# Row order of the expert weights and of the router's input, in a transformer block with 64 experts

## The chip, the core and the metric

The kernel runs on one core of a Trainium2 chip. The metric is the device time of one launch in microseconds (us). Before the change the median of three runs is 2787.24 us (2785.03 to 2787.96). The other cores of the chip are idle.

## What is computed

The input is 1024 tokens of 1024 numbers, all in float32. A first layer (an RWKV group, a sparse attention group and a memory group) and a second mixer (retention and convolution) are followed by a routed feed-forward layer, and only that layer is touched by the change. In short, for each token:

```
h2     = rms_norm(x1, norm2_w)                  # 1024 numbers
logits = h2 @ [router_g | router_e] + bias      # 8 group and 64 expert logits
e1, e2 = the two best experts of the best group, with two gates g1, g2
y      = sum over the two: g * ( silu(h2 @ w_gate[e]) * (h2 @ w_up[e]) ) @ w_down[e]
out    = rms_norm(x1 + y, final_norm_w)
```

`w_gate[e]` and `w_up[e]` are 1024 x 512, `w_down[e]` is 512 x 1024: each is 2 MB, and 64 experts have three each, 403 MB in all. With 2048 pairs of token and expert there are about 32 tokens to an expert, and a block holds up to 64.

## The kernel before, in words

The program is written by hand for each engine (`pe_...`, `act_...`, `dve_...`, `pool_...`, `sp_...`), with semaphores between them, and runs in stages. The change touches the last three.

**Router** (`dve_router`, `pe_router`). Token tile by token tile (8 tiles of 128) TensorE does the output projection of the mixer, VectorE adds it to the residual and writes the normalised tile `h2` (line 2439). SyncE stores `h2` to DRAM as `h2d`, each token as two rows of 512. TensorE transposes `h2` (line 2357) and multiplies it by the router weights `rw`. Line 2439 writes `h2` in a permuted order: of the 1024 numbers of a token, number `8 n + c` goes to place `128 c + n`. The slice `c` of 128 neighbours thus holds the numbers `c, 8 + c, 16 + c, ...`, which is the order in which the rows of the gate and up weights lie over the partitions: `(p c) n -> p (c n)` gives partition `p` the rows `8 p` to `8 p + 7`, one stretch of 16 KB in DRAM.

**Tables**. VectorE, TensorE and GpSimd build the lists of tokens of each expert.

**Experts** (`sp_experts`, `pe_experts`, `act_experts`, `dve_experts`, `pool_experts`). All loads of weights ("chunks" of 2 MB) are issued by SyncE in one order: gate, up, down of expert 0, then of expert 1, and so on, 192 chunks into 7 buffers. Chunk `k` waits until TensorE has finished with chunk `k - 7`, and the waits are taken in order, so that a chunk whose buffer is free waits behind one whose buffer isn't. The first two are issued in the router stage, five more when that stage's memory is free. GpSimd gathers the tokens of a block (`xg`, 64 tokens as 128 rows of 512) and scatters the results (`ys`). In each turn of its loop TensorE does, in this order:

- gate(e) and up(e) in `hidden`, 8 products each;
- `turn_x(e+1)`: four transposes of `xg`. The tile that is turned is the stationary operand, so each has one weight load (LDWEIGHTS) of 128 columns;
- down(e-1), 8 products;
- `turn_h(e)`: eight small products that turn the gate and the up result, `Gs[0]` and `Gs[1]`, which are again the stationary operand. A float32 product is run as two passes, each with a weight load, so these are 16 loads of 128 columns.

Between them ScalarE copies the gate result from PSUM to `Gs[0]` (line 2692, through the helper on line 229) and the turned tokens to `xT2` (line 2682, same helper), VectorE copies the up result to `Gs[1]` (line 2717). Both copies into `Gs` permute: number `4 n + c` goes to place `128 c + n` (`rows_of_wd`), which is the order of the rows of `w_down` over the partitions.

After the experts a stage ("over") handles blocks beyond 64, which are none here, and the final stage loads `yb`, adds, normalises and stores.

Of the kernel before, what the change touches and what calls it, by code (L numbers as in the profile page):

```python
# [14 lines left out]
ALU = mybir.AluOpType  # L15
# [141 lines left out]
def program(nc, inp, out):  # L157
# [48 lines left out]
    def s(name):  # L206
        if name not in sems:
            if name in LATER:
                old, left = LATER[name]
                sems[name] = Signal(s(old).sem, s(old).base + left)  # L210
            else:
                sems[name] = Signal(ctx.enter_context(nc.semaphore(name)), 0)
        return sems[name]
# [4 lines left out]
    def mm(pe, o, l, r, start, stop):  # L218
        return pe.e.matmul(o, l, r, start=start, stop=stop)  # L219
# [8 lines left out]
    def copy(act, o, i):  # L228
        return act.e.activation(o, i, ACT.Copy)  # L229
# [17 lines left out]
    def C(name, a=0, n=128):  # L247
        return con[:, CON[name] + a:CON[name] + a + n]

    ident = C("id")  # L250
# [292 lines left out]
    def four(a):  # L543
        return a.rearrange("p (a n) -> p a n", a=4)
# [1693 lines left out]
    xres = sb("xres", [128, 8, D], c=high)  # L2238
    NCH = 7
    wch = [sb(f"wch{i}", [128, 4096], c=high) for i in range(2)]  # L2240
# [34 lines left out]
    n2b = sb("n2b", [128, D], c=c8_)  # L2275
    rw = sb("rw", [128, 8, 72], c=c8_)
    rb_ = sb("rb_", [128, 72], c=c8_)
    junk5 = sb("junk5", [128, D], c=c8_)
    h2 = [sb(f"h2{i}", [128, D], c=c8_) for i in range(3)]
# [19 lines left out]
    def chunk_loaded(k):  # L2299
        return s(f"chunk_slot{k % NCH}"), 16 * (k // NCH + 1)  # L2300

    def sp_chunk(sp, k):
        if k >= NCH:
            e, n = (k - NCH) // 3, (k - NCH) % 3
            u = ps[("gate", "up", "down")[n], e]
            sp.wait_ge(u.full, u.v)
        e, n = k // 3, k % 3
        src = inp[("wg", "wu", "wd")[n]][e].rearrange("(p c) n -> p (c n)", p=128)
        sp.e.dma_start(wch[k % NCH], src).then_inc(chunk_loaded(k)[0].sem, 16)  # L2309

    def wo2_load(eng, first):
        for c in range(first, 8, 2):
# [6 lines left out]
    def h2_stored(j):  # L2319
        return s(f"h2_slot{j % 3}"), 16 * (j // 3 + 1)  # L2320
# [94 lines left out]
    def dve_router(dve):  # L2415
        dve.wait_ge(s("norm2_gain"), 16)
        dve.wait_ge(s("router_b"), 16)
        dve.wait_ge(s("con2"), 16)
        for j in range(8):
            m = small[:, 16 + j:17 + j]  # L2420
            dve.wait_ge(s(f"x{j}"), 32)
            for n in range(2):
                ns = slice(n * 512, (n + 1) * 512)
                u = ps["out2", j, n]
                dve.wait_ge(u.full, u.v)
                dve.e.tensor_tensor(xres[:, j, ns], xres[:, j, ns], u.t[:, :], ALU.add).then_inc(u.free.sem, 1)
            if j:
                dve_route(dve, j - 1)
            dve.wait_ge(s("res2_sq"), j + 1)
            dve.e.tensor_scalar(m, m, 1.0 / D, 1e-6, ALU.mult, ALU.add).then_inc(s("res2_mean").sem, 1)  # L2430
            dve.wait_ge(s("res2_root"), j + 1)
            dve.e.reciprocal(m, m).then_inc(s("res2_scale").sem, 1)
            dve.wait_ge(s("res2_scale"), j + 1)
            if j >= 3:
                dve.wait_ge(*h2_stored(j - 3))
                u = ps["h2T", j - 3, 1]
                dve.wait_ge(u.full, u.v)

            dve.e.scalar_tensor_tensor(h2[j % 3].rearrange("p (c n) -> p n c", c=8), xres[:, j, :].rearrange("p (n c) -> p n c", c=8),
                                       m, n2b.rearrange("p (n c) -> p n c", c=8), ALU.mult, ALU.mult).then_inc(s("h2").sem, 1)  # L2440
        dve_route(dve, 7)

    def dve_route(dve, j):
# [145 lines left out]
    Gs = [sb(f"Gs{i}", [128, 512], c=c11) for i in range(2)]  # L2589
# [13 lines left out]

    def turn_x(pe, o, x):
        for q in range(4):
            t = pe.e.transpose(o[:, q * 128:(q + 1) * 128], x[:, q * 128:(q + 1) * 128], ident)  # L2606
        return t

    def hidden(pe, o, w, xt_):
# [6 lines left out]

    def turn_h(pe, o, g):
        for c in range(4):
            t = mm(pe, o[:, c * 64:c * 64 + 64], g[:, c * 128:(c + 1) * 128], C("id2", 0, 64), True, True)
        return t  # L2620

    def rows_of_wd(u_):

        return u_.rearrange("p (n c) -> p c n", c=4)

    def down(pe, o, w, h_):
        for c in range(4):
# [10 lines left out]
    def sp_experts(sp):  # L2638
        for k in range(2, 3 * NEXP):
            sp_chunk(sp, k)  # L2640
# [35 lines left out]
    def act_turn_x(act, e):  # L2676
        u = ps["xT", "expert", e]
        act.wait_ge(u.full, u.v)
        if e >= 2:
            w = ps["up", e - 2]  # L2680
            act.wait_ge(w.full, w.v)
        copy(act, xT2[e % 2][:, :, :], four(u.t[:, :])).then_inc(u.free.sem, 1)

    def act_experts(act):
        act_turn_x(act, 0)
        for e in range(NEXP):
            u = ps["gate", e]
            act.wait_ge(u.full, u.v)
            if e:
                w = ps["hT", e - 1]  # L2690
                act.wait_ge(w.full, w.v)
            copy(act, four(Gs[0][:, :]), rows_of_wd(u.t[:, :])).then_inc(u.free.sem, 1)
            if e + 1 < NEXP:
                act_turn_x(act, e + 1)
            u = ps["hT", e]
            act.wait_ge(u.full, u.v)
            if e >= 2:
                w = ps["down", e - 2]
                act.wait_ge(w.full, w.v)
            act.e.activation(sg[e % 2][:, :, :], u.t[:, :].rearrange("p (a n) -> p a n", a=8)[:, 0:4, :],  # L2700
                             ACT.Silu).then_inc(s("gate_half").sem, 1)

    def dve_down(dve, e):
        u = ps["down", e]
        dve.wait_ge(u.full, u.v)
        if e >= 2:
            dve.wait_ge(*scattered(e - 2))
        dve.e.tensor_scalar(ys[e % 2][:, :], u.t[:, :], gat[:, e:e + 1], None, ALU.mult).then_inc(u.free.sem, 1)  # L2708

    def dve_experts(dve):  # L2710
        for e in range(NEXP):
            u = ps["up", e]
            dve.wait_ge(u.full, u.v)
            if e:
                w = ps["hT", e - 1]
                dve.wait_ge(w.full, w.v)
            dve.e.tensor_copy(four(Gs[1][:, :]), rows_of_wd(u.t[:, :])).then_inc(u.free.sem, 1)  # L2717
            if e:
                dve_down(dve, e - 1)
            u = ps["hT", e]  # L2720
            dve.wait_ge(s("gate_half"), e + 1)
            dve.e.tensor_tensor(sg[e % 2][:, :, :], sg[e % 2][:, :, :], u.t[:, :].rearrange("p (a n) -> p a n", a=8)[:, 4:8, :],
                                ALU.mult).then_inc(u.free.sem, 1)
        dve_down(dve, NEXP - 1)
# [38 lines left out]
    obank = ps.tiles  # L2763

    def sp_over(sp, n):
        sp.wait_ge(s("over_done"), n)
        for k_, name in enumerate(("wg", "wu", "wd")):
            v = sp.e.value_load(eid[n:n + 1, 0:1], min_val=0, max_val=NEXP - 1)
            src = inp[name][bass.ds(v, 1)]
            sp.e.dma_start(wch[k_], src.rearrange("a (p c) n -> p (a c n)", p=128)).then_inc(s(f"over_{name}").sem, 16)  # L2770

    def pool_over(pool, n):
        gather(pool, xg[0], NEXP + n).then_inc(s("over_x").sem, 16)
# [26 lines left out]
    def dve_over(dve, n):  # L2800
        dve.wait_ge(s("over_turned"), n + 1)
        dve.e.tensor_copy(xT2[0][:, :, :], four(obank[0][:, :])).then_inc(s("over_xT").sem, 1)
        dve.wait_ge(s("over_gate"), n + 1)
        dve.e.tensor_copy(four(Gs[0][:, :]), rows_of_wd(obank[1][:, :])).then_inc(s("over_gate_copied").sem, 1)
        dve.wait_ge(s("over_up"), n + 1)
        dve.e.tensor_copy(four(Gs[1][:, :]), rows_of_wd(obank[2][:, :])).then_inc(s("over_up_copied").sem, 1)
        dve.wait_ge(s("over_silu"), n + 1)
        dve.e.tensor_tensor(sg[0][:, :, :], sg[0][:, :, :], obank[3][:, :].rearrange("p (a n) -> p a n", a=8)[:, 4:8, :],
                            ALU.mult).then_inc(s("over_h").sem, 1)
        dve.wait_ge(s("over_down"), n + 1)  # L2810
        dve.e.tensor_scalar(ys[0][:, :], obank[4][:, :], gat[:, NEXP + n:NEXP + n + 1], None, ALU.mult).then_inc(s("over_y").sem, 1)
# [213 lines left out]
def layout(i):  # L3025
# [13 lines left out]
    a = {"x": i["x"][0], "mem": i["mem"][0]}  # L3039
# [27 lines left out]
    p, r = np.arange(128)[:, None], np.arange(128)[None, :]  # L3067
    for n in range(2):
        q = p % 64 + 64 * n
# [35 lines left out]
    a["n2"] = i["norm2_w_2"][0]  # L3105
    re = i["router_e_w_2"][0].transpose(1, 0, 2).reshape(1024, 64)
    rw = np.concatenate([i["router_g_w_2"][0], re], axis=1)
    a["rw"] = np.ascontiguousarray(rw.reshape(128, 8, 72))
    a["rb"] = np.concatenate([i["router_g_b_2"].reshape(-1), i["router_e_b_2"].reshape(-1)])
    a["wg"], a["wu"], a["wd"] = i["w_gate_2"][0], i["w_up_2"][0], i["w_down_2"][0]  # L3110
    a["fn"] = i["final_norm_w_2"]
# [1 line left out]
    p = np.arange(128)[:, None]  # L3113
# [30 lines left out]
```

## Time and profile before

| | us |
|---|---|
| median of three runs | 2787.24 |
| lowest and highest run | 2785.03, 2787.96 |
| time of the execution that was profiled | 2787.96 |
| its span in the trace | 2786.1 |

The profile page gives each engine's busy share (TensorE, "PE", 85%; its weight loads, "PEld", 55%; VectorE, "DVE", 28%; ScalarE, "ACT", 19%; GpSimd, "POOL", 21%) and, over 40 equal slices, what was busy when. One slice is 70 us, and the expert stage is the slices from 25 to 38. A busy share of TensorE says that products were in flight, not that it worked at its peak. The line "DMA" is the mean busy share of the core's 16 DMA engines; it can come out slightly over 1 where packets overlap. "L219" is line 219, the helper that issues nearly every product, and "L2309" the one that issues the chunks. Of shapes, `128*64 128x512` is a product with 128 rows and 64 columns of weights, through which 512 columns are moved. SPq, PEldq and the like are the queues of the engines.

### The profile page before, as it was taken

Reading aid. Unit: us, or ns where it says so; the run is one execution under the profiler, and the core shown is the slowest. Engines: PE = TensorE matmul, PEld = TensorE weight load, DVE = VectorE, ACT = ScalarE, POOL = GpSimd, SP = SyncE. Lnnn points to the kernel's source line nnn. Section 1 sums busy time; section 2 is a strip of 40 time slices with the busy share of each in tenths; the row PEclk is TensorE's granted clock in tenths of the full one; section 3 lists DMA queues with packets and bytes.
Section 4 is the critical chain, followed back from the end, with each engine's and each line's share of the span. In section 5 each row is a group of like instructions: output and inputs, shape, how many; then the busy total and the mean of one; then the engine's idle time right before and its main releaser. Section 6 shows DMA issues by size and latency. Waiting matters only on the chain. (4 is left out here: it accounts for less than half of the span.)

```text
span 2786.1 us, 42314 instructions
## 1 busy us (share of the span) xinstructions
PE 2370.5 (85%) x18624; PEld 1520.0 (55%) x18624; DVE 767.8 (28%) x1528; ACT 536.0 (19%) x1076; POOL 583.7 (21%) x366
## 2 busy tenths in 40 slices
PE   4899987888789999699999896988888888888881
PEld 4788865777567654488887454433333333333330
DVE  2311015553545533332323335111111111111114
ACT  2011123342255411111111121110010100100101
POOL 2433324331111111333322002111111111111113
PEclk9999988999799999899999997999999999999996
DMA  4122221002110011211111504899999999999994
GB/s 158 61 91 98 91 88 40 11 26 78 63 61 2 1 53 68 91 38 53 54 38 31 212 31 172 346 425 425 425 425 425 423 423 423 422 420 419 424 385 194
DMA packets 69647, 537.39 MB, mean 193 GB/s; under 512 B 13336, under 2 KB 13592, under 8 KB 43472
## 3 DMA queue, kind: packets, MB, share of 16 engines
q1 hardware_dynamic: 52720, 498.60, 43.6%
q10 hardware_dynamic: 6496, 19.19, 2.0%
q0 software_dynamic: 10240, 16.82, 1.6%
q8 instruction: 149, 2.44, 0.4%
q14 instruction: 42, 0.34, 0.0%
HBM read 503.08 MB, written 43.52 MB: 196 GB/s over the span
## 5 line engine op out<-in xcount | busy, mean ns | idle before, releaser
L219 PE MATMUL banks<-arena 64*64 64x64 f32 (+11 forms) x15392 | 1685.2, 346 | 271.3 <-DMA arena<-in_wu 84.5
L219 PEld LDWEIGHTS banks<-arena 64*64 64x64 f32 (+3 forms) x15392 | 953.2, 156 | 950.0 <-issue 684.1
L229 ACT ACTIVATE arena<-banks 128x512 f32<-128x512 f32 (+6 forms) x381 | 219.7, 587 | 1286.8 <-PE banks L219 561.5
L2600 POOL DMA_INDIRECT yb<-arena x64 | 65.1, 1018 | 841.2 <-DVE arena L2708 841.2
L2717 DVE COPY arena<-banks 128x512 f32<-128x512 f32 x64 | 44.3, 692 | 551.9 <-PE banks L219 551.9
L224 PE MATMUL banks<-r,w2s 128*128 128x512 f32 x448 | 177.4, 396 | 19.1 <-POOL w2s L1983 19.1
L224 PE MATMUL banks<-r,wlo 128*128 128x512 f32 x432 | 171.3, 397 | 7.2 <-POOL wlo L414 7.2
L225 PE MATMUL banks<-r,w2s 128*128 128x512 f32 x448 | 175.5, 392 | 0.0
L226 PE MATMUL banks<-r,w2s 128*128 128x512 f32 x448 | 175.1, 391 | 0.0
L226 PE MATMUL banks<-r,wlo 128*128 128x512 f32 x432 | 170.0, 394 | 0.0
L225 PE MATMUL banks<-r,wlo 128*128 128x512 f32 x432 | 169.8, 393 | 0.0
L1983 POOL TENSOR_TENSOR w2s<-arena,w2s 128x1024 fp32r<-128x1024 f32 x28 | 70.4, 2514 | 209.1 <-DVE w2s L1974 209.1
L2708 DVE TENSOR_SCALAR arena<-banks,arena 128x512 f32<-128x512 f32 x64 | 48.1, 751 | 222.3 <-PE banks L219 222.3
L224 PEld LDWEIGHTS banks<-r,w2s 128*128 128x128 f32 x448 | 84.9, 189 | 36.5 <-issue 19.4
L224 PEld LDWEIGHTS banks<-r,wlo 128*128 128x128 f32 x432 | 81.6, 189 | 25.9 <-POOL wlo L414 7.6
L226 PEld LDWEIGHTS banks<-r,w2s 128*128 128x128 f32 x448 | 84.8, 189 | 17.9
L225 PEld LDWEIGHTS banks<-r,w2s 128*128 128x128 f32 x448 | 84.9, 189 | 17.0
L1519 ACT ACTIVATE arena<-banks,arena 128x256 f32<-128x256 f32 (+4 forms) x160 | 76.4, 487 | 85.6 <-DVE arena L1498 43.7
L226 PEld LDWEIGHTS banks<-r,wlo 128*128 128x128 f32 x432 | 81.5, 189 | 19.2
L225 PEld LDWEIGHTS banks<-r,wlo 128*128 128x128 f32 x432 | 81.6, 189 | 18.7
L2700 ACT ACTIVATE arena<-banks 128x256 f32<-128x256 f32 x64 | 24.5, 383 | 314.5 <-PE banks L219 314.5
L1498 DVE TENSOR_REDUCE arena<-banks 128x1 f32<-128x512 f32 (+5 forms) x128 | 60.3, 510 | 73.5 <-PE banks L219 73.4
(240 smaller groups left out, 1527.5 us busy)
## 6 DMA issues: line engine op xcount, KB each, us to landing
arena<-in_wg SPq DMA_DIRECT2D x64, 2048.0 KB, 18.0
arena<-in_wu SPq DMA_DIRECT2D x64, 2048.0 KB, 22.9
arena<-in_wd SPq DMA_DIRECT2D x64, 2048.0 KB, 27.9
arena<-in_w SPq DMA_DIRECT2D x55, 512.0 KB, 3.3
spill<-arena SPq DMA_DIRECT2D x27, 512.0 KB, 2.6
arena<-spill SPq DMA_DIRECT2D x27, 512.0 KB, 5.5
arena<-yb SPq DMA_DIRECT2D x8, 1024.0 KB, 12.5
arena<-in_x SPq DMA_DIRECT2D x12, 512.0 KB, 4.9
```

What stands on the lines that cost most here:

```text
L219: return pe.e.matmul(o, l, r, start=start, stop=stop)
L224: pe.e.matmul(o, lh, rh, start=start, stop=False)
L225: pe.e.matmul(o, lh, rl, start=False, stop=False)
L226: return pe.e.matmul(o, ll, rh, start=False, stop=stop)
L229: return act.e.activation(o, i, ACT.Copy)
L1498: dve.e.tensor_reduce(o, i, AX.X, ALU.max, negate=True).then_inc(s("row_max").sem, 1)
L1519: t = act.e.activation(Pb[br][:, h, jj, 512 * x:512 * x + n], i, ACT.Exp, bias=mx[:, u % 4, 0, c:c + 1], accum_out=rs[:, u % 4, x, c:c + 1])
L1983: pool.e.tensor_tensor(wl[:, 1, :, :], w2r[n % 2][:, :, :], wl[:, 0, :, :].bitcast(F32), ALU.subtract).then_inc(s("w2_low").sem, 1)
L2600: return pool.e.indirect_dma_start(yb, bass.IndirectOffsetOnAxis(ap=six[:, col:col + 1].bitcast(U32), axis=0), src[:, :], None, bounds_che ...
L2700: act.e.activation(sg[e % 2][:, :, :], u.t[:, :].rearrange("p (a n) -> p a n", a=8)[:, 0:4, :], ACT.Silu).then_inc(s("gate_half").sem, 1)
L2708: dve.e.tensor_scalar(ys[e % 2][:, :], u.t[:, :], gat[:, e:e + 1], None, ALU.mult).then_inc(u.free.sem, 1)
L2717: dve.e.tensor_copy(four(Gs[1][:, :]), rows_of_wd(u.t[:, :])).then_inc(u.free.sem, 1)
```

## The change

Which DRAM row lies in which partition is changed for gate and up. Partition `p` now holds the rows `4 p` to `4 p + 3` and `512 + 4 p` to `512 + 4 p + 3`, two stretches of 8 KB (before: one of 16 KB). For `w_down` the rows stay where they were; the load is only written in another way. `h2` is now written in its natural order on line 2439, the router weights `rw` are laid out on the host to match, and the copies into `Gs` don't permute. In exchange the two turns on TensorE read every fourth column: `turn_x` takes `x[:, q:512:4]` and `turn_h` takes `g[:, c:512:4]` as stationary operand, where they took 128 neighbours. A step of 4 is 16 bytes in a partition. Number, kinds and order of the instructions are the same on every engine. The stage "over" is changed in the same way.

```diff
@@ sp_chunk
-        src = inp[("wg", "wu", "wd")[n]][e].rearrange("(p c) n -> p (c n)", p=128)
-        sp.e.dma_start(wch[k % NCH], src).then_inc(chunk_loaded(k)[0].sem, 16)
+        if n == 2:
+            src, dst = inp["wd"][e].rearrange("(p c) n -> p (c n)", c=4), wch[k % NCH]
+        else:
+            src = inp[("wg", "wu")[n]][e].rearrange("(h p q) n -> p h (q n)", h=2, q=4)
+            dst = wch[k % NCH].rearrange("p (h n) -> p h n", h=2)
+        sp.e.dma_start(dst, src).then_inc(chunk_loaded(k)[0].sem, 16)
@@ dve_router
-            dve.e.scalar_tensor_tensor(h2[j % 3].rearrange("p (c n) -> p n c", c=8), xres[:, j, :].rearrange("p (n c) -> p n c", c=8),
-                                       m, n2b.rearrange("p (n c) -> p n c", c=8), ALU.mult, ALU.mult).then_inc(s("h2").sem, 1)
+            dve.e.scalar_tensor_tensor(h2[j % 3][:, :], xres[:, j, :], m, n2b[:, :], ALU.mult, ALU.mult).then_inc(s("h2").sem, 1)
@@ turn_x
-            t = pe.e.transpose(o[:, q * 128:(q + 1) * 128], x[:, q * 128:(q + 1) * 128], ident)
+            t = pe.e.transpose(o[:, q * 128:(q + 1) * 128], x[:, q:512:4], ident)
@@ turn_h
-            t = mm(pe, o[:, c * 64:c * 64 + 64], g[:, c * 128:(c + 1) * 128], C("id2", 0, 64), True, True)
+            t = mm(pe, o[:, c * 64:c * 64 + 64], g[:, c:512:4], C("id2", 0, 64), True, True)
@@ act_experts
-            copy(act, four(Gs[0][:, :]), rows_of_wd(u.t[:, :])).then_inc(u.free.sem, 1)
+            copy(act, Gs[0][:, :], u.t[:, :]).then_inc(u.free.sem, 1)
@@ dve_experts
-            dve.e.tensor_copy(four(Gs[1][:, :]), rows_of_wd(u.t[:, :])).then_inc(u.free.sem, 1)
+            dve.e.tensor_copy(Gs[1][:, :], u.t[:, :]).then_inc(u.free.sem, 1)
@@ layout (on the host)
-    a["rw"] = np.ascontiguousarray(rw.reshape(128, 8, 72))
+    a["rw"] = np.ascontiguousarray(rw.reshape(8, 128, 72).transpose(1, 0, 2))
```

## Rows read from the trace of the kernel before

**Rows 1.** Busy time by window: us, each engine, granted clock, DMA share, GB/s

```profile
1740.00:1800.00 60.00, 60.00 (x300) 24.60 (x298) 7.40 (x12) 8.79 (x15) 6.85 (x7) 0.96 0.80 324
1900.00:2300.00 400.00, 344.83 (x1738) 144.84 (x1739) 47.44 (x77) 40.03 (x76) 51.21 (x50) 1.00 1.01 425
2300.00:2700.00 400.00, 344.21 (x1742) 145.76 (x1743) 47.66 (x77) 40.41 (x77) 52.23 (x51) 1.00 1.01 422
```

**Rows 2.** Chain that ended last, experts: start us, us, what

```profile
1808.07 3.65 PE banks L219 x16
...
2690.50 22.18 DMA arena<-in_wu
```

**Rows 3.** Waits, 1830 to 2700 us: us in total, times, longest

```profile
PE banks L219 <- DMA arena<-in_wu: 81.3, 54, 1.8
PE banks L219 <- DMA arena<-in_wg: 38.8, 56, 1.1
```

**Rows 4.** SyncE's chunk issues at the start of the experts: start us, us

```profile
1745.85 0.33 SPq L2309 DMA_DIRECT2D arena<-in_wu  x1
1749.28 0.33 SPq L2309 DMA_DIRECT2D arena<-in_wd  x1
1762.79 0.33 SPq L2309 DMA_DIRECT2D arena<-in_wg  x1
...
1775.90 0.33 SPq L2309 DMA_DIRECT2D arena<-in_wg  x1
...
1789.02 0.33 SPq L2309 DMA_DIRECT2D arena<-in_wg  x1
```

**Rows 5.** Busy time by window, as rows 1, between two of these issues

```profile
1757.00:1763.00 6.00, 6.00 (x31) 2.09 (x27) 0.90 (x2) 0.60 (x1) 0.00 (x0) 1.00 0.06 25
```

**Rows 6.** DMA queue of 1900:2700, then of 2744:2756: packets, MB, share of 16 engines

```profile
q1 hardware_dynamic: 22288, 324.59, 96.1%
q0 software_dynamic: 8220, 13.42, 4.5%
...
q1 hardware_dynamic: 705, 5.12, 101.3%
```

**Rows 7.** Window of chunks 0 and 1, then of the final loads, as rows 1

```profile
1564.00:1570.00 6.00, 6.00 (x15) 2.66 (x14) 3.06 (x5) 1.35 (x3) 0.00 (x0) 1.00 1.00 426
2744.00:2756.00 12.00, 0.00 (x0) 0.00 (x0) 7.55 (x3) 2.30 (x4) 11.76 (x5) 0.50 1.01 427
```

**Rows 8.** Weight loads and products around one `turn_x` and `turn_h`, timeline

```profile
2013.88 0.42 PEld L2606 LDWEIGHTS banks<-arena 128*128 128x128 f32 x4 [0.81 <-issue]
...
2014.47 5.58 PE L219 MATMUL banks<-arena 128*64 128x512 f32 x32
...
2018.05 1.86 PEld L219 LDWEIGHTS banks<-arena 128*128 128x128 f32 x16 [0.81 <-issue]
```

**Rows 9.** Small products by shape, windows 635:642, 681.6:684.8 and 670.8:674

```profile
L219 PE MATMUL banks<-arena 128*128 128x2 f32 x16 | 1.9, 252 | 0.5 <-ACT arena L1143 0.5
...
L219 PE MATMUL banks<-arena 64*64 64x1 f32 x114 | 3.5, 193 | 0.0
...
L219 PE MATMUL banks<-arena 64*64 64x63 f32 x62 | 3.6, 283 | 0.0
```

**Rows 10.** Chain, start of the experts; the granted clock until 1742 is in the second

```profile
1737.84 1.10 PE banks L2606 x4
...
1739.60:1742.00 2.40, 2.33 (x6) 0.77 (x8) 0.00 (x0) 0.02 (x1) 1.00 (x1) 0.50 0.18 56
```

**Rows 11.** Chain, end of the experts

```profile
2712.72 9.03 PE banks L219 x48
2721.75 0.02 issue
2721.78 0.39 ACT arena L2700
```

**Rows 12.** Lines 2439 and 2207: duration ns, min/median/max

```profile
L2439 DVE SCALAR_TENSOR_TENSOR arena<-arena x8: 1964/2002/2012, 1568.5 to 1691.0; 128x1024 f32<-128x1024 f32 x8
...
L2207 DVE SCALAR_TENSOR_TENSOR arena<-arena x4: 1283/1284/1289, 1260.1 to 1536.2; 128x1024 f32<-128x1024 f32 x4
```

**Rows 13.** Chain, last token tile of the router

```profile
1689.28 1.28 ACT L2399
1691.01 1.97 DVE arena L2439
1693.03 1.97 PE banks L2357 x8
```

**Rows 14.** Lines 229 (1900:2100) and 2717; line 2426 by shape

```profile
L229 ACT ACTIVATE arena<-banks x25: 597/597/597, 1905.1 to 2092.8; 128x512 f32<-128x512 f32 x25
...
L2717 DVE COPY arena<-banks x64: 691/692/693, 1749.4 to 2716.4; 128x512 f32<-128x512 f32 x64
...
L2426 DVE TENSOR_TENSOR arena<-arena,banks 128x512 f32<-128x512 f32 x10 | 6.9, 689 | 33.7 <-PE banks L219 33.7
```

More of the change, by code:

```diff
@@ L2618, in turn_h @@
         for c in range(4):
-            t = mm(pe, o[:, c * 64:c * 64 + 64], g[:, c * 128:(c + 1) * 128], C("id2", 0, 64), True, True)
+            t = mm(pe, o[:, c * 64:c * 64 + 64], g[:, c:512:4], C("id2", 0, 64), True, True)
         return t
-    def rows_of_wd(u_):
-        return u_.rearrange("p (n c) -> p c n", c=4)
     def down(pe, o, w, h_):
@@ L2769, in sp_over @@
             src = inp[name][bass.ds(v, 1)]
-            sp.e.dma_start(wch[k_], src.rearrange("a (p c) n -> p (a c n)", p=128)).then_inc(s(f"over_{name}").sem, 16)
+            if k_ < 2:
+                src, dst = src.rearrange("a (h p q) n -> p (a h) (q n)", h=2, q=4), wch[k_].rearrange("p (h n) -> p h n", h=2)
+            else:
+                src, dst = src.rearrange("a (p c) n -> p (a c n)", c=4), wch[k_]
+            sp.e.dma_start(dst, src).then_inc(s(f"over_{name}").sem, 16)
     def pool_over(pool, n):
@@ L2803, in dve_over @@
         dve.wait_ge(s("over_gate"), n + 1)
-        dve.e.tensor_copy(four(Gs[0][:, :]), rows_of_wd(obank[1][:, :])).then_inc(s("over_gate_copied").sem, 1)
+        dve.e.tensor_copy(Gs[0][:, :], obank[1][:, :]).then_inc(s("over_gate_copied").sem, 1)
         dve.wait_ge(s("over_up"), n + 1)
-        dve.e.tensor_copy(four(Gs[1][:, :]), rows_of_wd(obank[2][:, :])).then_inc(s("over_up_copied").sem, 1)
+        dve.e.tensor_copy(Gs[1][:, :], obank[2][:, :]).then_inc(s("over_up_copied").sem, 1)
         dve.wait_ge(s("over_silu"), n + 1)
```

## The prediction

> **What bounds the kernel now.** I read the windows first. From 1900 to 2700 us the 16 DMA engines are busy all the time (1.01 and 1.01, 425 and 422 GB/s) while TensorE is busy for 86% [rows 1]. The chain of waits says the same in order of time: it goes from one landing of up weights to TensorE's product with them and on to the next landing [rows 2]. TensorE waits for gate and for up in nearly every turn, 81.3 + 38.8 = 120.1 us over 56 turns, 2.1 us a turn [rows 3]. So the expert stage runs at the rate at which 403 MB come in, and a turn lasts what three chunks last. The product of expert 5 with its up weights starts at 1808.07 (its load is the one issued just behind the gate load at 1789.02), that of expert 63 at 2712.72 [rows 2, 4, 11]: 904.65 / 58 = 15.60 us a turn.
>
> The stage doesn't begin like that. Between 1740 and 1800 TensorE is busy throughout and DMA only for 0.80 [rows 1]. All seven buffers are full, and SyncE issues when down(0), down(1), down(2) are done: at 1762.79, 1775.90 and 1789.02 [rows 4], every 13.12 us. That is a turn when TensorE sets the pace, and the slack against the DMA's turn is 15.60 - 13.12 = 2.48 us. (The waits of rows 3 give 2.1; the ends of products are modelled, so I go by the issues.) Before 1762.79 the loads stop: in 1757 to 1763 the DMA share is 0.06 [rows 5]. From there on loads run to the end without a gap, as three chunks take longer than 13.12 us. Hence three places in which a change of this kind can move the end: the time of down(0), the length of a DMA turn, and what follows the last landing.
>
> **Part 1, two stretches of 8 KB for one of 16 KB.** Packets are one per stretch: 324.59 MB / 16384 B = 19812 packets of the 22288 on that queue; the rest are the little ones that signal an end [rows 6]. A gate or up chunk will have 256 packets for its 128, 8 more on each of 16 engines. Chunks 9 to 191 come after the gap, 122 of them gate or up: 976 more packets per engine. What one more costs I bound by spans and by rate. In the final stage only 8 KB packets move: 5.12 MB are 625 packets, which had 101.3% of 16 x 12 us = 194.5 us, 311 ns each [rows 6]. With chunks 0 and 1 alone on the queues 426 GB/s went through at a share of 1.00 [rows 7], which is 16384 B x 16 / 426 GB/s = 615 ns for a packet. By spans two halves take 2 x 311 - 615 = 7 ns more, so 976 x 7 ns = 6.8 us. By rate they take nothing: 427 GB/s with 8 KB against 426 with 16 KB [rows 7]. Bytes moved are what counts, and spans overlap (a share over 1 says so), so I go near the rate: +2 us, with 0 and +6.8 as ends. SyncE spends 0.33 us to issue a chunk [rows 4] and has 15 us a turn.
>
> The Trainium skill (DMA: Bandwidth & Descriptors, "Why small descriptors are slow (HBM only)") gives each packet a fixed overhead of about 3 cycles, at its fabric clock of 850 MHz an estimate of 3.5 ns and so 3.4 us for the 976. That lies inside the two ends.
>
> **Part 2, weight loads with a step of four.** This is the term that decides, and no load of this kind is in the trace. Neighbouring columns first: `turn_h` has 16 loads of 128 columns in 1.86 us, 116 ns each, `turn_x` four in 0.42 us, 105 ns each [rows 8]. The products behind them don't set this pace: with only 2 columns moved a pair of load and product still takes 1.9 / 16 = 119 ns [rows 9]. It is the load, at 0.9 ns a column. A moved column costs the same when neighbours are read: 16 products of 512 columns on two halves of the array side by side take 3.65 us [rows 2], 3.65 x 2 / (16 x 512) = 0.89 ns. Now the one stepped read that TensorE does: the compression's products (`kvc`, every 16th column, 63 of them) run in pairs, 62 in 3.6 us, so 116 ns a pair and 1.84 ns a column; with one column moved a pair takes 3.5 x 2 / 114 = 61 ns, so its own weight load isn't the limit [rows 9]. A stepped read of the moving operand is 2.1 times as slow. Taking this for the stationary one, a load of 128 columns goes from 116 to 232 ns: `turn_h` +1.86 us, `turn_x` +0.42 us, together +2.28 us a turn. The lower end is nothing. The upper end comes from VectorE: line 2439 writes with a step and takes 2002 ns for 1024 numbers, 1.96 ns each [rows 12], which for 128 columns is 250 ns, +2.7 us a turn. As I have a TensorE row I take it.
>
> The Trainium skill has a rule that speaks against the change (SBUF — State Buffer, "Door 1: The DMA port swizzle"): the memory has lines of 16 bytes, and an access that goes to a new line each time pays. A step of four float32 is a new line each time. The trace agrees for a step of 64 bytes (0.89 against 1.84 ns); no row shows one of 16.
>
> What it comes to on the path. With 2.28 us more TensorE's own turn is 15.40 us, under the DMA's 15.60 to 15.65. So 58 turns cost nothing, by a margin of only 0.2 us: the waits of rows 3 are what hides it, and they are all but used up. It does count where TensorE leads. Down(0) comes later by `turn_x(1)`, `turn_h(0)` and `turn_x(2)`, 0.42 + 1.86 + 0.42 = 2.7 us, and the loads start again as much later, since the DMA has nothing else to do in between. `turn_x(0)` runs at half clock, 1.10 us for four or 275 ns each [rows 10]; that is already slower than 232 ns, so nothing is added. At the end, `turn_h(63)` stands in the chain behind the last up product (9.03 us are up, down, turn) [rows 11]: +1.86 us.
>
> **Part 3, VectorE and ScalarE.** Line 2439 becomes the same operation as line 2207, 2002 to 1284 ns, -0.72 us in each of 8 tiles [rows 12]. In seven tiles TensorE is on the path with the next projection; in the last one the chain goes through it [rows 13]: -0.7 us. The copies into `Gs` read PSUM with a step of four now. ScalarE takes 597 ns for each of 25 copies, half of them the stepped ones and half the plain ones into `xT2`, and VectorE 692 ns against 689 for a plain read of the same size on line 2426 [rows 14]. So nothing goes there, and in the chain they are not (down(62) covers them); 0 us.
>
> **Sum.** +2 + 2.7 + 1.9 - 0.7 = +5.9 us on the profiled execution's 2787.96, so 2793.9. That execution was 0.7 us above the median of 2787.24, so the median should be 2793.1.
>
> **The rivals.**
> 1. *The step costs the weight loads nothing* (the stationary operand may be read ahead of use). For it: only the moving operand is seen with a step here, and at 64 bytes, not 16. Against: both operands run at the same 0.9 ns a column with neighbours, as if they shared a limit. Then +2 - 0.7 = +1.3, 2788.5.
> 2. *TensorE becomes the bound.* From 15.65 - 13.12 = 2.53 us a turn on, that is 126 ns more for each of 20 loads, every further 0.1 us costs 58 x 0.1 = 5.8 us. At VectorE's 1.96 ns a column a turn is 13.12 + 2.72 = 15.84 us: 0.24 x 58 = 14 us, with the start (3.3), the tail (2.1) and -0.7 about +19 (the packets then lie beside TensorE), so 2806. If a load took three times as long, 4.6 us a turn, it would be 2.1 x 58 = 120 us and 9 for start and tail, near 2916. Against it: the TensorE row says 2.1 times, just short.
> 3. *Faster: the halves are read better.* In the expert stage a 16 KB packet took 96.1% of 16 x 800 us / 19812 = 621 ns, while alone it took 615 [rows 6, 7]. It shares its engine with the gathers (4.5%) and a shorter packet may lose less to that and to the memory. If two halves take the 615 of a packet alone, the gain is 976 x 6 ns = 5.9 us; it decides only where the step is free as well: -5.9 - 0.7 = -6.6, so 2780.6. For it there is only the difference of 6 ns.
> 4. *Slower loads.* Two streams 1 MB apart may suit the memory worse than one. In the final stage nothing of the kind is seen. 2% on 122 chunks of 4.9 us (2.1 MB at 425 GB/s) would be +12, with the start, the tail and the router +16, about 2803.
>
> **How the numbers follow.** The forecast (twofold loads, DMA still the bound) has 0.42, rival 1 0.26, rival 2 0.18, rival 3 0.09, rival 4 0.05. What a measurement of this kernel can tell from no change is about 0.2%, 5.6 us, that is 2781.7 to 2792.8. The forecast stands right at that edge, its own range is 2791 to 2798 by the packets' ends, and I put 0.26 of its 0.42 above. Slower: 0.26 + 0.18 + 0.05 = 0.49. Same: 0.16 + 0.26 and a little of rival 3 = 0.43. Faster: 0.08. The range for 8 in 10 leaves out most of rival 3 and the far part of rival 2: 2785 to 2812.
>
> **What would show it.** Right: the stepped loads of `turn_h` take 3.7 us for 16 and those of `turn_x` 0.84 for four; the issue that was at 1762.79 comes 2.7 us later relative to the stage's start and the next two follow at some 15.4 us; TensorE's waits for gate and up fall from 2.1 us a turn to a few tenths; a DMA turn stays at 15.6; line 2439 takes 1.28 us. The step of part 2 is wrong if the 16 loads still take about 1.9 us, or over 4. The forecast is wrong if waits on weights vanish while the DMA share falls below 1 (rival 2), or if the rate in 1900 to 2700 differs from 423 GB/s by over 1% (rivals 3 and 4).

## The result, and the profile after

The changed kernel takes 2857.46 us (median of four runs, 2854.03 to 2865.12), before 2786.14 beside it: ratio 1.0262, 95% interval 1.0235 to 1.0287. That is 73 us slower by the ratio, 71 between the two medians. The profiled execution took 2856.57 us, its span is 2854.8. The forecast was 2793.1.

The windows, in the columns of [rows 1]: window, its length, busy time of the engines PE, PEld, DVE, ACT, POOL, then granted clock, DMA share and GB/s.

```profile
1740.00:1800.00 60.00, 60.00 (x254) 29.96 (x252) 6.31 (x11) 7.60 (x13) 6.16 (x6) 0.93 0.77 306
1900.00:2300.00 400.00, 400.00 (x1646) 191.40 (x1644) 44.73 (x72) 38.04 (x73) 49.14 (x48) 0.91 0.99 398
2300.00:2700.00 400.00, 400.00 (x1654) 191.82 (x1652) 45.41 (x73) 38.47 (x74) 49.16 (x48) 0.91 0.99 398
```

TensorE is busy all the time now, no longer for 86%, the rate has gone from 425 to 398 GB/s, and the granted clock is 0.91. The bound has passed from the DMA to TensorE: the chain is products only, and the waits of [rows 3] have no counterpart. Here is the chain after, start, us, what:

```profile
1956.40 16.18 PE banks L219 x64
1973.25 16.17 PE banks L219 x64
1990.11 16.18 PE banks L219 x64
2006.96 14.48 PE banks L219 x64
...
2022.12 15.81 PE banks L219 x64
2038.61 16.10 PE banks L219 x64
```

The 64 products of a turn take 16.2 us in most turns and 14.48 in one of six. The loads of weights inside two neighbouring turns, after (start, us, count):

```profile
2010.47 4.07 PEld L219 LDWEIGHTS banks<-arena 128*128 128x128 f32 x20 [0.81 <-issue]
...
2021.37 0.56 PEld L2608 LDWEIGHTS banks<-arena 128*128 128x128 f32 x4 [0.81 <-issue]
...
2025.63 4.22 PEld L219 LDWEIGHTS banks<-arena 128*128 128x128 f32 x20 [0.81 <-issue]
2030.46 0.24 PEld L219 LDWEIGHTS banks<-arena 128*64 128x64 f32 x2 [0.62 <-issue]
2031.32 0.24 PEld L219 LDWEIGHTS banks<-arena 128*64 128x64 f32 x2 [0.62 <-issue]
2032.17 0.16 PEld L219 LDWEIGHTS banks<-arena 128*64 128x64 f32 x2 [0.62 <-issue]
2032.62 0.14 PEld L219 LDWEIGHTS banks<-arena 128*64 128x64 f32 x2 [0.29 <-issue]
```

The stepped loads of `turn_h` (16, with four of the next product in the row) are near what was forecast. What follows them is new: the loads of the gate product come every 0.86 us until 2032.2 and every 0.43 from then on. Two windows of the same trace say why. The first begins in the stepped loads of this turn, the second lies over those of the turn before, which kept its clock:

```profile
2028.80:2032.20 3.40, 3.40 (x12) 1.44 (x13) 0.42 (x1) 0.38 (x1) 0.86 (x1) 0.50 0.99 363
...
2010.50:2014.50 4.00, 4.00 (x20) 3.93 (x20) 0.75 (x1) 0.04 (x1) 2.05 (x2) 1.00 0.80 270
```

Towards the end of the stepped loads the granted clock falls from 2.4 to 1.2 GHz (0.50), for about 3.4 us, and most of that falls on the dense products that come next. The Trainium skill (TensorE: Matmul & The Clock Gate, "Part 1: The HAM clock gate") describes a gate that passes all or half of the pulses by how busy the array has been; the two levels agree with the rows. Its section "HAM oscillation" has such falls come from waits for DMA. Here no wait comes before or in the fall (3.40 of 3.40 us busy), so a full busy share in the profile is no sign that the clock holds.

In SyncE's issues this is the turn, first before (the end of the experts; their start is in [rows 4]), then after:

```profile
2690.13 0.33 SPq L2309 DMA_DIRECT2D arena<-in_wg  x1
```

```profile
1761.98 0.37 SPq L2313 DMA_DIRECT2D arena<-in_wg  x1
...
1778.83 0.37 SPq L2313 DMA_DIRECT2D arena<-in_wg  x1
...
1795.68 0.37 SPq L2313 DMA_DIRECT2D arena<-in_wg  x1
...
2010.59 0.37 SPq L2313 DMA_DIRECT2D arena<-in_wg  x1
...
2025.74 0.37 SPq L2313 DMA_DIRECT2D arena<-in_wg  x1
...
2751.92 0.37 SPq L2313 DMA_DIRECT2D arena<-in_wg  x1
```

A turn with a whole fall in it is 16.85 us (1761.98 to 1778.83), one without is 15.15 (2010.59 to 2025.74). The 68.7 us between the spans lie so: up to the issue of chunk 9, -0.8; from there to chunk 15, two turns, 33.70 for 26.23 us, +7.5; the next 58 turns, 956.24 for 901.11 us, 16.49 for 15.54 each, +55.1; from the last of these issues to the end, 102.9 for 96.0, +6.9. This is a division by issues, not by causes. Before, the DMA share is already 1.00 from 1765 to 1805, while TensorE's turns are still 13.12 us, so those two turns are not what sets the end there. In the changed kernel TensorE sets the pace from chunk 9 on; its 60 turns between these issues take 989.9 us for 927.3 before.

### The profile page after: what moved, and what is told of

Read it like the earlier page. It is cut to its first block and busy times, and to the rows that moved or that the text cites. A ratio compares the mean times of both kernels' runs of the same rounds, so it can differ in the third digit from the quotient of the medians.

```text
span 2854.8 us, 42314 instructions
## 1 busy us (share of the span) xinstructions
PE 2563.5 (90%) x18624; PEld 1660.1 (58%) x18624; DVE 765.0 (27%) x1528; ACT 536.5 (19%) x1076; POOL 583.2 (20%) x366
## 5 line engine op out<-in xcount | busy, mean ns | idle before, releaser
L219 PE MATMUL banks<-arena 64*64 64x64 f32 (+11 forms) x15392 | 1873.0, 365 | 147.8 <-ACT arena L229 21.3
L219 PEld LDWEIGHTS banks<-arena 64*64 64x64 f32 (+3 forms) x15392 | 1085.2, 167 | 879.3 <-issue 735.1
L2720 DVE TENSOR_TENSOR arena<-arena,banks 128x256 f32<-128x256 f32 x64 | 27.0, 421 | 227.4 <-ACT arena L2698 227.4
```

## The experiments

Theory A: the piece of stepped loads makes TensorE's clock fall, and the turn with the fall is longer than the DMA's. Theory B: the clock falls because TensorE never waits. Theory C: the halves of 8 KB are what slows the stage. Every ratio is against the kernel before.

**1. The hidden turn taken back, the rest of the change kept.**

```diff
-            t = mm(pe, o[:, c * 64:c * 64 + 64], g[:, c:512:4], C("id2", 0, 64), True, True)
+            t = mm(pe, o[:, c * 64:c * 64 + 64], g[:, c * 128:(c + 1) * 128], C("id2", 0, 64), True, True)
# and both copies into Gs through rows_of_wd again
```

> The changed kernel with only the turn of the hidden rows taken back: neighbouring columns as stationary operand and permuting copies, as before; the halves of 8 KB, the natural h2 and the stepped turn of x stay. Theory A (TensorE's granted clock falls in a stretch of nothing but stepped weight loads, and the slow stretch after it makes TensorE the bound): the long stretch is gone, the clock stays at 1.00 in 1900 to 2700, a turn is 15.6 us by DMA, time 2785 to 2790. Theory B (the clock falls because TensorE never waits): TensorE waits again (its own turn is 13.3 us), so also 2785 to 2790. Theory C (the halves of 8 KB slow the loads): at least half of the 71 us stays, 2820 or more, and the rate is 398 GB/s with waits on weights.

Measured: 2795.67 us, ratio 1.0040 (1.0027 to 1.0053), clock 1.00. The window, columns as above:

```profile
1900.00:2300.00 400.00, 344.43 (x1727) 147.42 (x1724) 47.29 (x76) 40.02 (x76) 51.07 (x50) 1.00 1.01 420
```

Theory C falls: of 73 us 62 go with the hidden turn. The forecast for A and B was some 5 us too low: the rate is 420 GB/s against 425, and runs 5 and 6 show that the halves cost more than I had put.

**2. Only the hidden turn stepped.**

```diff
-            t = mm(pe, o[:, c * 64:c * 64 + 64], g[:, c * 128:(c + 1) * 128], C("id2", 0, 64), True, True)
+            t = mm(pe, o[:, c * 64:c * 64 + 64], g[:, c:512:4], C("id2", 0, 64), True, True)
# in the kernel before, with plain copies into Gs
```

> The kernel before with only the turn of the hidden rows stepped and its copies plain; loads, h2 and the turn of x as before. Theory A: 16 stepped loads in about 3.8 us, TensorE's own turn 15.0 us at full clock, but the clock falls for some 3.4 us in most turns, which then last 16.7 us, on average 16.4; time 2845 to 2860. Theory B: the same if TensorE's waits vanish, but at 15.0 us a turn against 15.6 there would be waits left and no fall: about 2791. Theory C: 2791, no change but start and tail.

Measured: 2851.19 us, ratio 1.0238 (1.0215 to 1.0261). The window:

```profile
1900.00:2300.00 400.00, 400.00 (x1658) 190.61 (x1660) 45.15 (x73) 38.27 (x74) 50.62 (x50) 0.91 0.99 401
```

One line of the change makes nearly all of the loss, as A has it. Its own turn without a fall is 15.06 us (issues at 1767.79 and 1782.85), under the DMA's. I had taken this as a case against theory B, but it isn't one: in the first turns TensorE leads and never waits, so B too can have the clock fall there, and once it falls the waits don't come back. Runs 3, 4 and 7 decide on B.

**3. All stepped loads kept, the hidden turn in two pieces.** Half of the down product stands between them.

```diff
-                pe_down(pe, e - 1)
+                down(pe, d.t, wch[(3 * e - 1) % NCH], sg[(e - 1) % 2], 0, 2)
...
             turn_h(pe, u.t[:, 0:256], Gs[0])
+            if e:
+                down(pe, d.t, wch[(3 * e - 1) % NCH], sg[(e - 1) % 2], 2, 4).then_inc(d.full.sem, 1)
```

> The changed kernel, every stepped load kept, but the turn of the hidden rows is split: its first eight loads stand between the two halves of the down product, the other eight behind it. Theory A: the stretches of stepped loads are 1.9 us and not 3.8, the clock stays at 1.00 (or falls in few turns), TensorE's own turn is 15.2 to 15.4 us, DMA is the bound again: 2790 to 2798. Theory B: TensorE still hardly waits, the clock still falls: 2850 or more. If it is the amount of stepped loading in a turn and not its being in one piece, also 2850.

Measured: 2801.78 us, ratio 1.0070 (1.0048 to 1.0093). The window, and the loads of one turn:

```profile
1900.00:2300.00 400.00, 398.17 (x1744) 193.46 (x1740) 47.77 (x77) 40.41 (x77) 53.11 (x52) 1.00 1.01 421
```

```profile
2005.05 2.21 PEld L219 LDWEIGHTS banks<-arena 128*128 128x128 f32 x12 [0.81 <-issue]
...
2008.93 2.21 PEld L219 LDWEIGHTS banks<-arena 128*128 128x128 f32 x12 [0.81 <-issue]
```

The same work in the same number of instructions, with half of the down product now between the two pieces: the clock is back at 1.00, DMA is the bound, and 54 us are won back (ratio 1.0070 for 1.0262). TensorE is busy for 398 of 400 us and keeps its clock, which speaks against B. At 15.46 us a turn of its own TensorE has only just room, and the time is 4 us over what was expected.

**4. Dense work added to the kernel before**, so that TensorE never waits.

```diff
     def down(pe, o, w, h_):
+        for n in (0, 1) * 3:
+            mm(pe, o[64 * n:64 * n + 64, :], h_[:, 0, :], w[:, n * 512:n * 512 + 512], True, True)
```

> The kernel before with six more products of 512 columns ahead of each down product (they repeat its first slice and are overwritten): TensorE's own turn goes from 13.12 to 15.86 us, above the DMA's 15.60, without any stepped load. Theory A: the clock stays at 1.00, a turn is 15.86 us, and the time is 15 us for the turns, 3 for the start and 5 for the two last down products above before: 2805 to 2815. Theory B (TensorE that never waits gets a lower clock): clock about 0.91, a turn of 17 us, 2870 to 2890.

Measured: 2805.50 us, ratio 1.0077 (1.0054 to 1.0099). The window:

```profile
1900.00:2300.00 400.00, 400.00 (x2044) 163.94 (x2042) 47.60 (x77) 39.84 (x76) 52.23 (x51) 1.00 1.01 419
```

400 of 400 us busy at clock 1.00: theory B is refuted. The turn is 15.69 us (15.86 expected), and with TensorE as the bound at full clock the kernel is 21.5 us slower than before, not 73.

**5. The halves alone.** `h2` is permuted within each half (line 2439 becomes two instructions), so both turns read neighbours.

```diff
+            src = inp[("wg", "wu")[n]][e].rearrange("(h p q) n -> p h (q n)", h=2, q=4)
+            dst = wch[k % NCH].rearrange("p (h n) -> p h n", h=2)
# (cut) and line 2439, the router weights and the stage "over" to match
```

> The kernel before with the two stretches of 8 KB alone: h2 is written permuted within each half of 512 numbers (two instructions) and the router weights laid out to match, so both turns read neighbouring columns as before. If the halves are what the kernel with the plain hidden turn loses against before (11.7 us, its rate 419 for 423 GB/s): 8 to 12 us slower than before, 2792 to 2796, rate 419 GB/s. If the stepped turn of x has a part in it: 4 to 8 us slower.

Measured: 2794.38 us, ratio 1.0030 (1.0018 to 1.0042), that is 5.0 to 11.7 us. The window:

```profile
1900.00:2300.00 400.00, 341.95 (x1716) 143.19 (x1714) 46.57 (x75) 40.05 (x76) 51.20 (x50) 0.99 1.01 421
```

**6. Two packets from one stretch of 16 KB**, places in the buffer exchanged.

```diff
+            sp.e.dma_start(wch[k % NCH].rearrange("p (h n) -> p h n", h=2)[:, ::-1, :],
+                           src.rearrange("p (h n) -> p h n", h=2)).then_inc(chunk_loaded(k)[0].sem, 16)
# (cut) for gate and up only; the slices in the product are exchanged to match
```

> The kernel before with each partition's 16 KB of gate and up weights taken as two packets of 8 KB from the same 16 KB of DRAM, their places in the buffer exchanged (and the slices in the product to match), h2 and turns as before. Theory P (it is the number of packets): the same loss as with the halves, 8 to 12 us. Theory M (it is that the two packets come from places 1 MB apart): no loss, within 3 us of before.

Measured: 2792.10 us, ratio 1.0025 (1.0013 to 1.0037), 421 and 418 GB/s in the two windows, the same as in run 5. The loss comes with twice the packets at half the size; places 1 MB apart add nothing that shows. The traces say the same: from the issue of chunk 9 to TensorE's last product it is 963.6 us before, 972.0 in run 5 and 972.2 in run 6. Run 1 with its stepped turn of x lies inside the same interval, so that turn costs too little to be seen here.

**7. The hidden turn done twice with neighbouring columns.**

```diff
-        for c in range(4):
+        for c in (0, 1, 2, 3) * 2:
```

> The kernel before with the turn of the hidden rows done twice over: 32 weight loads of neighbouring columns with 64 columns moved behind each, 3.7 us in one piece, as long as the 16 stepped loads. If the clock falls because small products stand in one piece for that long: it falls in most turns here too, a turn is 16.5 us, about 2850. If it is how little is moved in that piece (a product of 64 columns every 116 ns here, every 240 ns with the step): the clock stays at 1.00, TensorE's own turn is 15.0 us, DMA stays the bound, 3.7 us for start and tail: 2788.

Measured: 2790.36 us, ratio 1.0015 (1.0005 to 1.0025), clock 1.00. The loads, then the window:

```profile
2001.58 3.91 PEld L219 LDWEIGHTS banks<-arena 128*128 128x128 f32 x36 [0.81 <-issue]
```

```profile
1900.00:2300.00 400.00, 388.20 (x2157) 185.63 (x2153) 48.03 (x77) 40.66 (x77) 51.18 (x50) 1.00 1.01 424
```

A piece as long, of the same kind of product, with twice as many of them: no fall. In the first turns TensorE leads here as well (14.90 us a turn, busy for 100 of 100 us from 1760 to 1860) and the clock is 1.00, once more against B. So a long piece of small products doesn't bring the fall; 16 loads at 240 ns in one piece do.

Is it the step or the slowness of the loads? No run has slow loads without a step. But the kernel before has two falls of its own in 1900 to 2700, at 2178 and 2396, each behind `turn_h` with neighbouring columns and a wait of 1 us for gate weights. Here is the first, products and then a window:

```profile
2171.19 5.58 PE L219 MATMUL banks<-arena 128*64 128x512 f32 x32
2177.83 8.52 PE L219 MATMUL banks<-arena 128*64 128x512 f32 x30 [1.06 <-DMA arena<-in_wg]
...
2178.00:2180.00 2.00, 2.00 (x6) 0.63 (x5) 0.00 (x0) 0.00 (x0) 0.80 (x1) 0.55 0.96 410
```

So a fall needs no stepped load. These two cost nothing that shows, as the DMA is the bound there.

**8. Work added to the changed kernel**, between the two halves of the hidden turn.

```diff
             turn_h(pe, u.t[:, 0:256], Gs[0])
+            for n in (0, 1) * 2:
+                mm(pe, u.t[64 * n:64 * n + 64, 256:512], C("id2", 0, 64), Gs[0][:, 0:256], True, True)
```

> The changed kernel with work added: between the eight stepped loads of the gate's turn and the eight of the up's turn four products of 256 moved columns (about 1 us, overwritten afterwards). Theory A (the piece of stepped loads makes the clock fall): the clock stays at 1.00, a turn is 15.2 + 1.0 = 16.2 us against 16.49 on average for the changed kernel, and the time is lower although more is done: 2835 to 2845. If filling doesn't keep the clock: 17.5 us a turn, 2910 or more.

Measured: 2844.30 us, ratio 1.0208 (1.0193 to 1.0223). The window:

```profile
1900.00:2300.00 400.00, 400.00 (x1866) 199.75 (x1864) 45.41 (x73) 39.09 (x74) 49.13 (x48) 1.00 1.00 404
```

More work and less time than the changed kernel (its interval is 1.0235 to 1.0287), at clock 1.00 and 16.3 us a turn: theory A's most particular claim holds. The gain is 13 us between the medians, 15 by the ratios.

**9 and 10. The step itself: every second and every third column**, one run each. Only the time is read: these turn partly other columns than the layer needs.

```diff
-            t = mm(pe, o[:, c * 64:c * 64 + 64], g[:, c:512:4], C("id2", 0, 64), True, True)
+            t = mm(pe, o[:, c * 64:c * 64 + 64], g[:, c:c + 256:2], C("id2", 0, 64), True, True)
# and g[:, c:c + 384:3]
```

> The kernel before with plain copies and a turn of the hidden rows that reads every second column (8 bytes apart); it turns columns of which half are the wrong ones, so the results of the experts are not the reference's, only the times are read. If what costs is a new line of 16 bytes for each number: two numbers still share a line, 16 loads take 1.9 us as with neighbours, clock 1.00, about 2787. If any step costs: 3.8 us, the clock falls, about 2850.

> The same with every third column (12 bytes apart), again with the wrong columns. By lines of 16 bytes three numbers of four start a new line or are alone in it: between 2.5 and 3.8 us for the 16 loads. If a step of any size costs twice: 3.8 us and the clock falls, 2850.

Measured: 2787.70 and 2788.49 us, with 2790.55 for the kernel before beside them. The loads of 128 columns of line 219 from 1830 to 2700, for step 2 and then step 3. The total busy time stands first, then the mean ns of one, which is longer than total by number because loads overlap:

```profile
L219 PEld LDWEIGHTS banks<-arena 128*128 128x128 f32 x896 | 110.8, 197 | 45.4 <-issue 45.4
```

```profile
L219 PEld LDWEIGHTS banks<-arena 128*128 128x128 f32 x896 | 161.0, 262 | 45.4 <-issue 45.4
```

896 are 56 turns: 1.98 us a turn with step 2 and 2.88 with step 3. With step 4 (run 2) 848 loads have 201.9 us, 3.81 us a turn. The Trainium skill's rule on lines of 16 bytes (SBUF — State Buffer, "Door 1: The DMA port swizzle") fits: a step is nearly free while two numbers share a line. An estimate from these runs: at 238 / 128 = 1.86 ns for each 16 bytes touched, and never under the 116 ns of neighbours, steps of 2, 3 and 4 (a half, three quarters and one line a number) would take 119, 179 and 238 ns; 124, 180 and 238 were measured. With step 3 the windows' clock is 0.98 and 0.97, so it falls in some turns there too (13 of the 56), and the time doesn't show it, because TensorE's own turn (14.13 us, 15.83 with a fall) leaves room.

**11. The stepped hidden turn alone, in two pieces**: run 2 with the edit of run 3.

```diff
-                pe_down(pe, e - 1)
+                down(pe, d.t, wch[(3 * e - 1) % NCH], sg[(e - 1) % 2], 0, 2)
```

> The kernel before with the hidden turn stepped and split in two by half of the down product; loads in one stretch of 16 KB, h2 and the turn of x as before. It is the kernel with the stepped hidden turn alone (67 us slower than before) with nothing changed but the place of eight loads. If the fall of the clock is all that those 67 us are made of, and the stepped loads themselves stay under the DMA's turn: clock 1.00, TensorE's own turn 15.3 us against the DMA's 15.54, 3 to 7 us slower than before for start and tail, 2790 to 2795. If the stepped loads cost of themselves: more than 10 us slower.

Measured: 2799.34 us, ratio 1.0048 (1.0031 to 1.0064). Its issues of a gate load:

```profile
1773.05 0.33 SPq L2309 DMA_DIRECT2D arena<-in_wg  x1
1788.40 0.33 SPq L2309 DMA_DIRECT2D arena<-in_wg  x1
1803.76 0.33 SPq L2309 DMA_DIRECT2D arena<-in_wg  x1
...
2703.68 0.33 SPq L2309 DMA_DIRECT2D arena<-in_wg  x1
```

53 of run 2's 67 us go with the place of eight loads. The 58 turns behind 1803.76 take 15.52 us each, as before (15.54). What is left, 13 us (8.6 to 17.8), is more than I expected. In the profiled run it is 14.2 us, and its trace divides them so. The first gather of the experts starts 5.4 us later (1739.73 for 1734.29); what lies ahead of it the edit doesn't touch, so this part is no cost of the steps, and gathers of the other traces start between 1729.6 and 1736.7. From there to the issue of chunk 9 it is 33.3 us for 28.5, +4.8, and from chunk 9 to TensorE's last product 967.4 for 963.6, +3.9, of which the last `turn_h` is 1.9. A part of the 4.8 is once more a fall:

```profile
1754.00:1758.00 4.00, 4.00 (x21) 3.93 (x21) 0.51 (x1) 1.88 (x3) 0.00 (x0) 1.00 1.02 438
1758.00:1762.00 4.00, 4.00 (x12) 1.21 (x14) 0.42 (x1) 0.38 (x1) 0.00 (x0) 0.57 0.96 410
```

The loads of the first window are those of `turn_h(0)`. No down product stands with it that could divide it, so this one turn is still in one piece, and the fall behind it is the only one until TensorE's last product. (Run 3 has the same undivided piece and no fall there; not every such piece brings one, as in the changed kernel.) Down(0), which now stands behind half of `turn_h(1)`, is later too.

No run is shown to be faster than the kernel before. Runs 9 and 10 lie 2.9 and 2.1 us under the one run beside them, which says nothing; run 7 is the nearest of the others.

## Why the prediction was wrong

**The step that failed** is in part 2, "What it comes to on the path": that with TensorE's own turn at 15.40 us under the DMA's 15.60 the 58 turns cost nothing. The working up to there holds, at full clock even with something to spare: `turn_h` took 3.81 us (forecast 3.72), `turn_x` 0.56 (0.84), a turn 15.15. But 15.40 was worked out at the clock of [rows 1], 1.00, as if a slower load left the clock as it was. It doesn't. The sparse piece brings a fall in five of six turns, a turn with a whole fall takes 1.7 us more, and the average of 16.49 is 0.95 us above what these turns took before (15.54): 58 times that is 55 us. Runs 3, 8 and 11 take the falls away with the stepped loads of `turn_h` in place. In runs 3 and 11 most of the loss goes with them, and in run 8 the falls' part of it does, less what the added work takes.

**Rival 2** named the right bound for the wrong reason. It let TensorE take over from 126 ns more for each load; the loads of `turn_h` stayed at about 122 ns more (1.95 us over 16), just under, and TensorE took over all the same. Its 2806 would have been too little; no case held a term for the clock, and so the range ended at 2812.

**The start and the end.** +2.7 us for the issue of chunk 9 was about right (30.8 us behind the first gather for 28.5). That the next two turns don't count where the DMA is the bound is borne out too, within 2 us: in runs 7 and 11 these turns are 3.6 and 4.5 us longer than before, and yet from chunk 9 to TensorE's last product the two take 967.6 and 967.4 us for 963.6, of which the longer last `turn_h` is 1.9. In the changed kernel TensorE is the bound, so every turn counts from the first: 1033.0 us for that stretch, 69.4 more, against the +1.9 that was forecast for it beside the packets.

**The packets** were the right mechanism with the size too small: +2 us forecast, 0 and 6.8 as ends, and the halves alone measure 8.4 (5.0 to 11.7). The rate I went by [rows 7] can't tell 1%: its window of 6 us gives 436 GB/s when it starts 1 us earlier and 423 when it starts 2 us earlier. The spans, which gave 7 ns for each packet more, were nearer: 8.4 us over 976 is 8.6 ns. In the long windows of the expert stage the rate fell by 1%. Whether 8 KB packets would lose as much without gathers beside them stays open. That the 1 MB between the halves does harm, rival 4, is not borne out (run 6); rival 3, a gain by the halves, is refuted.

**Rival 1**, a free step, is refuted: 240 ns for a load against 116. **VectorE's and ScalarE's part** came as said: line 2439 (2442 now) takes this, and the copies are as long as before.

```profile
L2442 DVE SCALAR_TENSOR_TENSOR arena<-arena x8: 1283/1285/1286, 1565.5 to 1688.4; 128x1024 f32<-128x1024 f32 x8
```

What stays open is what exactly brings the fall. It comes behind 16 loads at 240 ns in one piece in most turns, behind 16 at 180 ns in 13 of 56, and now and then behind 16 at 116 ns with a wait of 1 us after them. Behind 32 loads at 116 ns, or 8 at 240, in one piece it didn't come.

## What to carry to other kernels

When an edit makes TensorE's small products slower, the cover of a waiting TensorE isn't measured by its idle time alone. Look at what the granted clock does over and behind the sparse piece, and price the turn at the lower level for as long as a fall lasts in your trace (here 3.4 us, which cost 1.7). If slow loads can't be avoided, break them up with dense products that are there anyway; here moving eight loads won back 53 us. A step that puts each float32 into its own 16 bytes doubled a weight load here (116 to 238 ns), a step of two did next to nothing (124 ns).

## What the runs showed of the hardware that was not expected

- TensorE's granted clock falls to 0.50 for about 3.4 us while the engine is busy without a break: in the window 2028.80 to 2032.20 of the changed kernel, 3.40 of 3.40 us busy.
- Added work can save time: run 8 does about 1.1 us more in each of 64 turns and is 13 us faster than the changed kernel (2844.30 for 2857.46).
- A float32 weight load of 128 columns takes 116, 124, 180 and 238 ns with steps of 1, 2, 3 and 4 (1.86, 1.98, 2.88 and 3.81 us for 16).
- Halving the packets of gate and up from 16 to 8 KB costs 1% of the rate in the expert stage (425 to 421 GB/s), 8.4 us or 8.6 ns for each packet more.
- The kernel before has falls of its own (2178 and 2396, granted clock 0.55 in 2178 to 2180) behind neighbouring loads and a wait of 1 us.
